# Output weights split during the values' projection and fetched back; two output projections inside the last head pair

## What is computed

```
qkv = x @ w_in
o_a = windowed attention (+-128 tokens, 8 query heads on 2 key heads, a sink logit per head)
o_b = three dilated attentions (128,1), (512,4), (2048,16), merged by their softmax denominators
mix = concat(rms_norm(o_a, norm_a), rms_norm(o_b, norm_b)) @ w_out
x1  = layer_norm(alpha * x + mix)
y   = layer_norm(alpha * x1 + moe(x1))     # 16 experts in 4 groups, top 2 of one group, a shared expert
```

## Time and profile before

| what | us |
|---|---|
| median of 3 runs (lowest, highest) | 1287.08 (1285.97, 1288.6) |
| span of the profiled execution | 1287.2 |
| PE busy | 1217.7 (95%) |
| DVE busy | 732.8 (57%) |
| ACT busy | 578.9 (45%) |
| POOL busy | 197.5 (15%) |
| values' projection | 0 to 110 |
| four head pairs | 144 to 660.3 |
| output projection, merge, first norm | 660.3 to 812 |
| experts | 812 to the end |

### The profile page before, as it was taken

The page is one execution under the profiler, slowest core; times in us unless marked ns, Lnnn a source line. Parts: engine busy times, 40 slices in busy tenths (PEclk is TensorE's granted clock), DMA queues, the critical chain, the costliest instruction groups (busy, mean ns, idle before and its releaser), DMA issues.

```text
span 1287.2 us, 22113 instructions
## 1 busy us (share of the span) xinstructions
PE 1217.7 (95%) x8077; PEld 1091.6 (85%) x8077; DVE 732.8 (57%) x1790; ACT 578.9 (45%) x1416; POOL 197.5 (15%) x244
## 2 busy tenths in 40 slices
PE   7999999999999999998798999998799999999992
PEld 6998798888888888886677888897699999999892
DVE  3111455655655555556767887448566556666377
ACT  3221344444444444445543433220366666667464
POOL 0000001200210021011101212000213333333222
PEclk9999999999999999999898999899799999999996
DMA  5444654374537344565264343432899999999773
GB/s 185 160 128 128 170 142 100 78 187 91 135 80 181 95 108 94 142 148 165 76 203 161 133 148 107 166 146 66 252 295 275 286 293 274 273 275 296 196 290 131
DMA packets 157986, 220.69 MB, mean 171 GB/s; under 512 B 40608, under 2 KB 110496, under 8 KB 157856
## 3 DMA queue, kind: packets, MB, share of 16 engines
q1 hardware_dynamic: 147168, 180.80, 47.1%
q0 software_dynamic: 8192, 29.36, 10.5%
q10 hardware_dynamic: 2544, 9.44, 1.8%
HBM read 139.05 MB, written 50.63 MB: 147 GB/s over the span
## 4 chain that ended last, share of the span: by engine, by line
PE 83%; DVE 6%; ACT 3%; issue 3%; DMA 2%; DVEq 1%; POOL 1%; ACTq 1%; SPq 0%; POOLq 0%
PE bank L849 19%; PE bank L851 18%; PE bank L850 18%; PE bank L956 9%; PE bank L843 5%; PE bank L943 5%; PE bank L932 4%; PE bank L933 3%; PE bank L1076 2%; ACT b_work L1329 1%; DVE w_o L1689 1%; DMA acc_scratch<-d_work,dstc 1%; ACT w_o L1344 1%; DVE d_work L2098 1%; DMA xg<-x_scratch,idc 1%
## 5 line engine op out<-in xcount | busy, mean ns | idle before, releaser
L1329 ACT ACTIVATE b_work<-b_work 128x256 f32<-128x256 f32 (+3 forms) x288 | 148.0, 514 | 245.3 <-DVE b_work L1670 245.0
L849 PE MATMUL bank<-xgT_hi,w_gu_hi 128*128 128x224 f32 (+1 forms) x704 | 197.9, 281 | 5.2 <-ACT d_work L1562 3.1
L850 PE MATMUL bank<-xgT_lo,w_gu_hi 128*128 128x224 f32 (+1 forms) x704 | 196.5, 279 | 0.0
L851 PE MATMUL bank<-xgT_hi,w_gu_lo 128*128 128x224 f32 (+1 forms) x704 | 196.4, 279 | 0.0
L1679 DVE COPY b_work<-bank 128x256 f32<-128x256 f32 (+2 forms) x256 | 112.6, 440 | 116.0 <-PE bank L943 115.4
L849 PEld LDWEIGHTS bank<-xgT_hi,w_gu_hi 128*128 128x128 f32 x704 | 136.9, 194 | 7.4 <-issue 3.9
L2189 POOL CAST Q<-Q 128x512 fp32r<-128x512 f32 x48 | 52.9, 1135 | 575.9 <-DVE w_k_lo L1636 342.7
L850 PEld LDWEIGHTS bank<-xgT_lo,w_gu_hi 128*128 128x128 f32 x704 | 137.0, 195 | 0.7
L851 PEld LDWEIGHTS bank<-xgT_hi,w_gu_lo 128*128 128x128 f32 x704 | 136.9, 194 | 0.0
L943 PE MATMUL bank<-keep,b_work 128*128 128x128 f32 x608 | 115.7, 276 | 13.0 <-ACT b_work L1329 13.0
L943 PEld LDWEIGHTS bank<-keep,b_work 128*128 128x128 f32 x608 | 79.4, 140 | 50.8 <-ACT b_work L1329 22.5
(11 more groups left out here) (210 smaller groups left out, 2843.0 us busy)
## 6 DMA issues: line engine op xcount, KB each, us to landing
d_work<-in_w_gate SPq DMA_DIRECT2D x32, 512.0 KB, 8.7
d_work<-in_w_up SPq DMA_DIRECT2D x32, 512.0 KB, 9.5
d_work<-in_w_down SPq DMA_DIRECT2D x16, 1024.0 KB, 9.4
Q<-stage_hi SPq DMA_DIRECT2D x96, 128.0 KB, 2.4
Q<-stage_lo SPq DMA_DIRECT2D x96, 128.0 KB, 2.4
o_scratch<-b_work SPq DMA_DIRECT2D x36, 264.0 KB, 3.2
c_work<-o_scratch SPq DMA_DIRECT2D x12, 792.0 KB, 5.2
raw_w<-in_w_in SPq DMA_DIRECT2D x26, 256.0 KB, 4.3
```

Of the source, the lines that this page charges most:

```text
L849: nc.tensor.matmul(o, w_hi, x_hi, start=first, stop=False)
L850: nc.tensor.matmul(o, w_hi, x_lo, start=False, stop=False)
L851: return nc.tensor.matmul(o, w_lo, x_hi, start=False, stop=last)
L1329: nc.scalar.activation(prob[:, u % 2, 0:n], prob[:, u % 2, 0:n], ACT.Exp, scale=-1.0, bias=o[:, HD:HD + 1], accum_out=o[:, HD + 1:HD + 2])\
```

## The change

`w_out` is loaded, split and scaled in the values' projection, in tiles 4 to 11: SP's `load_wo(k)` is two DMAs of 64 rows each (0.5 MB together), ACT's `wo_high(k)` follows the copies of tile k+4, DVE's `wo_low(k)` the transposes of x of tile k+5, and SP's `store_wo(k)` writes both parts (1 MB) to `wo_scratch`. `load_small` moves from tile 9 to tile 4, since the gains are needed. In the last pair ACT issues eight DMAs of 1 MB (`wo_back`, units 14 to 37), which fetch the split weights into `w_o`. The constants are gone (`warm`). Four tiles are merged in the pair (`MERGES`, with the units of ACT's squares and scaling in `SQUARES` and `SCALED`), two are transposed (`OT_UNITS` 55 and 67), tile 0's 16 steps stand in units 58 to 65, two in each, the first six of tile 1 in units 69 to 71, the residual of tile 0 in unit 66 and its statistics in 67. After the pair PE does the other 10 steps of tile 1 around `ot(2)`, then `ot(3)`, then goes on from `op(2)`. The buffers of the last two stages lie elsewhere: `raw_gu`, `raw_d` and `slab` are tensors of their own, and `raw_o` is gone. The diff, cut to what moves work:

```diff
-OP_UNIT = 58
-OP_UNITS = 14
-WARM = range(35, 55)
-WARM_BANK = 6
-OT0 = 10752
+WO_LOADS = (14, 16, 18, 20, 31, 33, 35, 37)
+MERGES = (46, 51, 56, 61)
+SQUARES = (51, 56, 61, 66)
+SCALED = (53, 58, 67, 70)
+OT_UNITS = (55, 67)
+OP_PLAN = {58 + n // 2: tuple((0, m) for m in (n, n + 1)) for n in range(0, 16, 2)}
+OP_PLAN.update({69 + n // 2: tuple((1, m) for m in (n, n + 1)) for n in range(0, 6, 2)})
+OP_REST = 6
...
+            def load_wo(k):
+                if k == 0:
+                    sp.wait_ge(S["wv_made"], KD)
+                if k > 1:
+                    sp.wait_ge(S["wo_lo"], 2 * k - 2)
+                for c in range(2):
+                    row = 256 * c + HD * k if k < 4 else P * k + HD * c
+                    sp.dma_start(wo_raw[k % 2][HD * c:HD * c + HD, :], w_out[row:row + HD])\
+                      .then_inc(S["wo_ld1" if k % 2 else "wo_ld0"], 16)
+            def store_wo(k):
+                sp.wait_ge(S["wo_lo"], 2 * k + 2)
+                for part in range(2):
+                    sp.dma_start(wo_d[:, (2 * k + part) * D:(2 * k + part + 1) * D], wo_s[part])\
+                      .then_inc(S["wo_st"], 16)
...
             for t in range(4, TILES):
                 store_v(t - 4)
                 load_x(t)
+                if t == 4:
+                    load_small()
+                if t >= 7:
+                    store_wo(t - 7)
+                if t >= 5:
+                    load_wo(t - 5)
                 if t == 8:
                     load_qa(0, 1)
-                if t == 9:
-                    load_small()
             for t in range(TILES - 4, TILES):
                 store_v(t)
+                if t == TILES - 4:
+                    store_wo(5)
+                    load_wo(7)
+                if t == TILES - 3:
+                    store_wo(6)
+            store_wo(7)
...
-                if last:
-                    sp.wait_ge(S["proj_made"], PRE + GROUPS * i + 2)
-                    for c, part in enumerate((w_out[0:256], w_out[256:512])):
-                        sp.dma_start(raw_o[HD * c:HD * c + HD, 0:4, :],
-                                     part.rearrange("(i p) n -> p i n", p=HD)).then_inc(S["wo_loaded"], 16)
...
+                    for t in range(2):
+                        sp.dma_start(odt[t], od_t[t]).then_inc(od_ld[t], 16)
                     dup_pair(5, i)
+                    for t in range(2):
+                        sp.dma_start(xr[:, t, :], x_t[t]).then_inc(xr_ld[t], 16)
...
-            sp.dma_start(xr[:, 0, :], x_t[0]).then_inc(xr_ld[0], 16)
...
+            for c in range(3):
+                sp.wait_ge(o_st[c], 16 * 3 * PAIRS + 16)
+            for half in range(2):
+                load_raw_gu(ws_gate, ws_up, half)
+            load_raw_d(ws_down)
+            c_step(1, 1, lambda d: True)
...
-            def op_first(n):
+            def op_early(t, n):
                 k, c = n % KD, n // KD
                 if n == 0:
-                    pe.wait_ge(S["oT_lo"], 1)
-                if c == 0:
-                    pe.wait_ge(S["wo_lo"], 2 * k + 2)
-                last = three(bank[6 + c][:], oT0_hi[:, k * P:k * P + P], oT0_lo[:, k * P:k * P + P],
+                    pe.wait_ge(S["oT_lo"], t + 1)
+                if t == 0 and n in (0, 4):
+                    pe.wait_ge(S["wo_back1" if n else "wo_back0"], 64)
+                a = t * D + k * P
+                last = three(bank[6 + c][:], oT_hi[:, a:a + P], oT_lo[:, a:a + P],
                              w_o[:, k, 0, 512 * c:512 * c + 512], w_o[:, k, 1, 512 * c:512 * c + 512],
                              k == 0, k == KD - 1)
                 if n == 2 * KD - 1:
                     last.then_inc(S["op_made"], 1)
...
-                    if last and g in WARM:
-                        warm(i, 1 if PLAN_LAST.get(g) else 2)
-                    if last and g == OT_UNIT:
+                    if last and g in OT_UNITS:
                         pe.wait_ge(S["proj_ready"], PRE + GROUPS * i + LAST_GROUPS)
-                        ot(0, 0, bank[6:8])
-                    if last and OP_UNIT <= g < OP_UNIT + OP_UNITS:
-                        op_first(g - OP_UNIT)
+                        ot(OT_UNITS.index(g), OT_UNITS.index(g), bank[6:8])
+                    for t, n in OP_PLAN.get(g, ()) if last else ():
+                        op_early(t, n)
...
-            ot(1, 1, bank[2:4])
-            for n in range(OP_UNITS, 2 * KD):
-                op_first(n)
-            ot(2, 0, bank[4:6])
-            for t in range(1, 4):
+            for n in range(OP_REST, 2 * KD):
+                if n == 3 * KD // 2:
+                    ot(2, 0, bank[4:6])
+                op_early(1, n)
+            ot(3, 1, bank[2:4])
+            for t in range(EARLY_OP, 4):
                 c_step(t, t % 2, lambda d, t=t: 0 <= t + d < TILES, t)
             with pe.Fori(0, TILES // 2 - 3) as i:
...
+            def wo_high(k):
+                if k == 0:
+                    act.wait_ge(S["gains_ld"], 48)
+                act.wait_ge(S["wo_ld1" if k % 2 else "wo_ld0"], 32 * (k // 2) + 32)
+                if k > 0:
+                    act.wait_ge(S["wo_st"], 32 * k)
+                for c in range(2):
+                    w = slice(512 * c, 512 * c + 512)
+                    nc.scalar.activation(wo_s[0][:, w].bitcast(FP32R), wo_raw[k % 2][:, w], ACT.Copy,
+                                         scale=gains[:, k:k + 1]).then_inc(S["wo_hi"], 1)
...
+            def wo_back(k):
+                if k == 0:
+                    act.wait_ge(S["wo_st"], 32 * KD)
+                at = slice(2 * k * D, 2 * k * D + 2 * D)
+                act.dma_start(plain(w_o_t[:, at]), wo_d[:, at]).then_inc(S["wo_back1" if k >= 4 else "wo_back0"], 16)
...
-                    if last and g in WO_UNITS:
-                        wo_high(WO_UNITS.index(g))
-                    if last and g == OT_UNIT + 1:
-                        oT_high(0, 0, bank[6:8], oT0_hi)
+                    if last and g in WO_LOADS:
+                        wo_back(WO_LOADS.index(g))
+                    if last and g - 1 in OT_UNITS:
+                        t = OT_UNITS.index(g - 1)
+                        oT_high(t, t, bank[6:8])
                     for t, m in enumerate(MERGES if last else ()):
                         if g == m + 1:
                             merge_exp(t)
-                        if g == m + 5:
+                        if g == SQUARES[t]:
                             squares(t, t % 2, x1s[:, 1, 0:512])
-                        if g == m + 7:
+                        if g == SCALED[t]:
                             scaled(t, t % 2)
                     if g % 4 == 3:
...
+            def wo_low(k):
+                for c in range(2):
+                    w = slice(512 * c, 512 * c + 512)
+                    dve.wait_ge(S["wo_hi"], 2 * k + c + 1)
+                    V.scalar_tensor_tensor(wo_s[1][:, w].bitcast(FP32R), wo_raw[k % 2][:, w], gains[:, k:k + 1],
+                                           wo_s[0][:, w], ALU.mult, ALU.subtract).then_inc(S["wo_lo"], 1)
             for t in range(2, TILES):
                 xt(t)
                 if t == 6:
                     w_split(0, w_k)
+                if t >= 5:
+                    wo_low(t - 5)
...
-                    if last and g in WO_UNITS:
-                        wo_low(WO_UNITS.index(g))
-                    if last and g == OT_UNIT + 1:
-                        oT_low(0, 0, bank[6:8], oT0_hi, oT0_lo)
+                    if last and g - 1 in OT_UNITS:
+                        t = OT_UNITS.index(g - 1)
+                        oT_low(t, t, bank[6:8])
+                    if last and g == RES_UNIT:
+                        residual(0, 0, 16, bank[6:8])
+                    if last and g == RES_UNIT + 1:
+                        ln1_stats(0, 0)
...
```

185 lines of the change are left out of this document (84 added, 101 removed).

## The result

The change is slower: 1314.02 us (median of 4 runs, 1313.3 to 1314.9) for 1287.03, a ratio of 1.0208 (95% interval 1.0194 to 1.0222), 27 us more. The forecast was 1292, with 1279 to 1300 as the range for 8 in 10. The profiled execution spans 1312.0 us for 1287.2, 24.8 more.

A forecast was written before the change was run, and what follows sets the result against it. TensorE was taken as the bound (83% of the chain), with multi-engine chains and a DMA landing setting some stretches. Terms +2.0 (last pair), 0 (behind it) and 3 (values' projection) gave 5 us on 1287.2, so 1292; range 1279 to 1300.

The forecast's parts named there:

- The eight fetches: Last pair, units 14 to 37: eight 1 MB fetches issued by ACT cost nothing, first used in unit 58.
- the four rivals: Whole kernel: faster (.29), values' projection bound by DMA (.11), gain and loss cancel (.18), clock falls to half (.05).
- Units 36 to 45 and 46 to 57: Last pair: split leaves the path, 12.5 us for 21.6, 9.1 less; then merges, 26 for 29.4, 3.4 less.
- Units 58 to the pair's end: Last pair, units 58 to 71: added output steps, residual and tile 1's transposes, 38.6 us for 24.1, 14.5 more.
- two bouts at half clock: Units 58 to 71: slow matmuls after PE stops, 2.4 us each, one early, one behind the second stop (units 67, 68).
- Behind the pair: Pair's end to third output tile: nothing gained, since tile 4's heads land 20.6 us after the end; 36.2 for 35.9.
- Its bound of 12 us less: Pair's end to third output tile: the gain if PE's own work, some 22.5 us, alone set the end.
- Values' projection: Tiles 7 to 11: added w_out traffic needs 8.8 us DMA per 7.9 us tile; 3 more, bounds 0 and 9.
- The 13 us by which halves of 64 rows might have slowed the stage: Values' projection: by the skill's rule on 64-row halves load_wo costs up to twice, some 13 us greater, time 1305.
- Constants: Last pair: removing the constant matmuls got no separate term; a clock well below .86 from unit 46 would refute the forecast.
- Rival (d): Last pair: without constants PE falls to half clock from the merging units through the output steps, 1303; chance .05.
- Rival (a): Mainly behind the pair: faster, heads of tile 4 land earlier, values' stage hides its DMAs, 1281; chance .29.

The follow-up runs named there:

- The run with the heads first: Changed kernel with SP issuing tile 4's heads ahead of the shared expert's 3 MB of weights, ACT waiting for those one step later: 1305.7, 8.4 less.
- The run of the kernel before with the heads first: Kernel before the change with tile 4's heads issued ahead of the shared expert's weights, ACT's wait one step later: 1288.1 for 1287.6, ratio 1.0003.
- the run without the path: Changed kernel without w_out's loads, splits, stores and fetches, GpSimd writing a constant into w_o: 1292.7, 3.8 less than with only the fetches left out.
- the new kernel: Changed kernel with the pair's end in old order, fetches and scaling re-placed, gains in tile 4, other small tables in tile 9: 1283.4.

## Why the prediction was wrong

The sign was right and the size was not: 5 us forecast, 25 in the profiled execution, 27 in the medians. Without the fetches the same kernel is 7.9 us slower than before in the profiles, so the other terms together were right within 3 us, though not each of them. Term by term:

- **The eight fetches: 0 forecast, 17.5 measured.** This is the step that failed. Its cover was raw_o's load: DMA share 1.03 while PE was busy 8.00 of 8.00. The row is right and says too little. That load stood in SP's own queue, behind the copies of one wave and ahead of the next: SP issued nothing from 559.1 to 567.7 us. The fetches go out from ACT at fixed units and meet the waves. The kernel before had a row that warned: the store of heads issued at 584.15, right behind 2 MB of `raw_o`, took 9.2 us to land for 3.2 usual, and nothing waited for it. I had written what would happen if the cover gave way ("the copies of keys and queries come late and projection groups with them"), and gave it neither a price nor a chance; none of the four rivals was it. What should have been read is when the copies are issued and how soon PE uses them, not whether PE was busy under a full DMA share.
- **Units 36 to 45 and 46 to 57: 9.1 and 3.4 less forecast, 8.6 and 1.3 less measured** (without fetches, by the forecast's own bounds: biases 38 to 48 take 12.8 us for 21.5, and 48 to 60 take 28.1 for 29.4). The first is right in mechanism and size: units of 0.8 to 1.3 us stand where 2.37 stood, and PE's waits for ACT are gone there. The second was sized at 26 and is 2.1 longer.
- **Units 58 to the pair's end: 14.5 more forecast, 10.9 measured** (bias 60 to the end: 35.4 us for 24.5, and 38.6 in the sum; from bias 59 on it is 11.7). The stops at the end were where the sum had them: 2.52 us for the residual and 3.81 for the low part of the transposes, with half clock behind. The first of its two bouts at half clock (2.4 us) did not come; the matmuls behind the first stop run at full clock:

```profile
644.68 0.51 PE L875 MATMUL bank<-w_o,oT_hi 128*128 128x512 f32 x1 [0.99 <-DVE oT_lo L1776]
645.49 0.39 PE L875 MATMUL bank<-w_o,oT_hi 128*128 128x512 f32 x1
```

  The two errors, 2.1 in the term above and 3.6 here, went against each other by luck.
- **Behind the pair: 0 forecast, 1.8 less measured.** The mechanism holds: the heads of tile 4 landed 704.5 - 684.1 = 20.4 us after the pair's end (20.6 forecast), PE stood 6.8 us, and output tile 3 began 33.9 after it (36.2 in the sum, which counted 2.4 us of half clock ahead of that step; the slow matmuls came behind it, and 1.9 of the 2.8 us in the table's last line are theirs). Its bound of 12 us less does not come out of its own terms, 35.9 less 22.5 is 13.4; it enters no sum. The run with the heads first confirms it with 8.4 us. The run of the kernel before with the heads first adds what I had not seen: there both bounds were level.
- **Values' projection: 3 more forecast, 3.8 measured** by the run without the path. The size is right and the form is not. By its own sign the forecast had tiles 7 to 11 longer than 7.9 us each; of these one was (9.2), the others kept 7.9 with the DMA engines at .99, so 8.8 us of DMA a tile was an over-estimate. The other loss is in tile 4 (9.9), where the tables are. The 13 us by which halves of 64 rows might have slowed the stage did not come.
- **Constants: 0, and 0 measured** in the kernel before. No run puts them back into the changed one, whose units are shorter: its clock was .79 from 617 to 641 us, where the forecast named "well below .86" as a sign of being wrong, so whether they would win part of the 2.1 us above stays open. Rival (d) has its premise right (the clock falls) and its price wrong: the merging units of the kernel before do not wait for PE, and the changed kernel's units with two output steps kept the full clock (matmuls of 0.39 us). The Trainium skill's rule in "TensorE: Matmul & The Clock Gate", section "A second HAM failure mode: psum-queue depth-cycling", weighed in the forecast, is borne out as to the clock, .76 and .67 in the run without constants, and moves no time here.
- **Rival (a)**, faster by an early landing, was wrong: the landing kept its place. The 1.4 us in pairs 0 to 2 and the last 0.9 behind output tile 3 were not forecast, and no run isolates them.

By whole parts the medians give a sum that closes (each run has its own median of the kernel before, and these lie within 1.5 us of one another): 1287 before; 12 less for the split kept in scratch memory, together with merges that begin earlier and no constants (1274.8); 21 more for the fetches' places and ACT's wait behind GpSimd (1295.6; in the profiles some 15 and 4); 18 more for the new end of the pair (1314.0). Each part is one edit of several lines, and only the constants' share in it, nothing, has a run of its own.

## What to carry to other kernels

A large transfer is free or dear by what is issued beside it: before moving one to another queue, list the small transfers of that stretch with their issue times and their users, and place the large one in the gaps. Moving work ahead of a boundary pays only where the stretch it leaves has no other bound; look for a landing that keeps its distance to the boundary. And an engine that is busy but not waited for (PE of the kernel before without the constants, at a lower clock) can be slower at no cost.

## What the runs showed of the hardware

- A copy of 128 KB took 2.4 us alone and up to 11.0 beside 1 MB transfers from another engine's queue. The Trainium skill, "DMA: Bandwidth & Descriptors", section "Queues, rings and completion order", says that each DMA engine takes turns between the queues by the packet. No run shows the turns. The trace fits them as far as it goes: from 588 to 612 us ACT's queue moved 4.19 MB in 576 packets and SP's 1.32 MB in 1168, so a packet of the fetches was on average over six times as long.
- A store of 264 KB took 9.2 us beside a load of 2 MB from the same queue, for 3.2 usual.
- The small tables, under 0.3 MB, cost nothing in tile 9 of the kernel before, and in other places more: 1.0 us in tile 4 without w_out's path, 1.6 to 2.3 with it and 6.7 once, 7 over two tiles in tile 7, 12 over two in tile 9 of the new kernel. Their many small packets may be the ground; this is not shown, since no run changes the packets and keeps the place.
- Without constants the granted clock was .76 and .67 for 51 us, for 1.00 and .86 with them, and the time was the same (ratio 0.9999, 0.9987 to 1.0011).
